# Taking the products of constants out of TensorE's waits in a two-block transformer kernel

## The reference, cut to what matters

```python
def hybrid_layer(xl, xc, ...):            # li = 0 with both streams, li = 1 ends the context stream
    hl = rmsnorm(xl, norm1_g) * (1 + sc1) + sh1
    # projections, q/k/v, rope ...
    a_l = mla_latent(...)                  # 6 heads
    b_l = swa_latent(...)                  # 6 heads
    xl = xl + g1 * (concat([a_l, b_l, cv_l]) @ w_o)
    xl = xl + g2 * ec_ffn(rmsnorm(xl, norm2_g) * (1 + sc2) + sh2, router_w, w_gate, w_up, w_down)

def ec_ffn(h, router_w, w_gate, w_up, w_down):
    aff = softmax(h @ router_w)            # 256 tokens x 16 experts
    top_aff, idx = lax.top_k(swapaxes(aff, 1, 2), 32)   # each expert picks its 32 tokens
    xg = h[idx]
    hid = silu(xg @ w_gate) * (xg @ w_up)
    # (hid @ w_down) * top_aff, added back to the tokens that were picked
```

## Time and profile before

| what | us |
|---|---|
| median of 3 runs | 2224.35 |
| lowest, highest | 2220.94, 2224.48 |
| the profiled execution | 2227.25 |
| its span, from the first to the last instruction | 2225.5 |
| TensorE busy in the span | 2066.0 (93%) |
| granted clock, mean over the span | 0.972 |

### The profile page before, as it was taken

The page is one execution under the profiler, slowest core; times in us unless marked ns, Lnnn a source line. Parts: engine busy times, 40 slices in busy tenths (PEclk is TensorE's granted clock), DMA queues, the critical chain, the costliest instruction groups (busy, mean ns, idle before and its releaser), DMA issues.

```text
span 2225.5 us, 32706 instructions
## 1 busy us (share of the span) xinstructions
PE 2066.0 (93%) x14137; PEld 1603.4 (72%) x14137; DVE 917.5 (41%) x1882; ACT 447.4 (20%) x984; POOL 86.3 (4%) x87
## 2 busy tenths in 40 slices
PE   6999999999899998667999999999999998999998
PEld 3444586555565476545878878899987788889998
DVE  2137723232326632113445423466514544146662
ACT  3004512111122421001223112100003411121001
POOL 1000010000000000000001100000000011000000
PEclk9999999999999999779999999999999999999999
DMA  9750633999922879997432214455543221244462
GB/s 369 250 202 25 211 127 118 395 424 426 400 77 78 303 296 388 416 416 291 148 107 103 76 64 142 148 178 158 159 151 121 97 93 68 86 151 165 157 166 82
DMA packets 186768, 435.69 MB, mean 196 GB/s; under 512 B 6362, under 2 KB 77954, under 8 KB 171010
## 3 DMA queue, kind: packets, MB, share of 16 engines
q1 hardware_dynamic: 185488, 431.19, 52.7%
q10 hardware_dynamic: 1138, 2.41, 0.3%
HBM read 432.53 MB, written 1.05 MB: 195 GB/s over the span
## 4 chain that ended last, share of the span: by engine, by line
PE 84%; DMA 8%; DVE 3%; ACT 2%; issue 1%; SPq 1%; DVEq 0%; ACTq 0%
PE bank L284 80%; DMA arena<-in_exp_w_up 3%; DMA ring<-in_exp_w_up 2%; PE bank L604 2%; PE bank L873 2%; DMA cst<-in_ada_w 1%; DMA ring<-in_exp_w_gate 1%; DMA cst<-in_exp_w_up 1%; SPq L3006 1%; ACT h L727 0%; ACT arena L827 0%; DVE arena L822 0%; PE bank L1452 0%; PE bank L1500 0%; DVE x L1381 0%
## 5 line engine op out<-in xcount | busy, mean ns | idle before, releaser
L284 PE MATMUL bank<-h,ring 128*128 128x256 f32 (+2 forms) x3360 | 744.6, 380 | 16.2 <-ACT arena L658 5.1
L284 PEld LDWEIGHTS bank<-h,ring 128*128 128x128 f32 x3360 | 595.5, 192 | 147.9 <-issue 68.3
L284 PE MATMUL bank<-arena 128*128 128x128 f32 (+13 forms) x3496 | 453.5, 328 | 40.4 <-DMA arena<-in_exp_w_gate 10.2
L284 PEld LDWEIGHTS bank<-arena 128*128 128x128 f32 (+5 forms) x3496 | 340.3, 171 | 131.4 <-issue 63.6
L284 PE MATMUL bank<-arena,ring 128*128 128x128 f32 (+1 forms) x1704 | 267.9, 317 | 1.0 <-PE bank L284 1.0
L284 PEld LDWEIGHTS bank<-arena,ring 128*128 128x128 f32 x1704 | 245.9, 191 | 19.6 <-PE bank L284 1.8
L827 ACT ACTIVATE arena<-bank 128x256 f32<-128x256 f32 (+4 forms) x227 | 100.5, 461 | 526.1 <-PE bank L284 497.2
L822 DVE COPY arena<-bank 128x512 f32<-128x512 f32 (+6 forms) x90 | 50.8, 566 | 242.0 <-PE bank L284 161.0
L284 PE MATMUL bank<-ring,arena 128*64 128x256 f32 (+1 forms) x1472 | 113.6, 348 | 20.8 <-DMA ring<-in_exp_w_up 13.3
L284 PEld LDWEIGHTS bank<-ring,arena 128*64 128x64 f32 (+1 forms) x1472 | 78.8, 130 | 58.1 <-DMA ring<-in_exp_w_up 16.8
L284 PE MATMUL bank<-h,arena 128*128 128x128 f32 (+2 forms) x704 | 109.9, 330 | 2.6 <-ACT arena L1491 2.6
(11 more groups left out here) (362 smaller groups left out, 1741.2 us busy)
## 6 DMA issues: line engine op xcount, KB each, us to landing
ring<-in_w_in SPq DMA_DIRECT2D x32, 2048.0 KB, 7.8
ring<-in_exp_w_up SPq DMA_DIRECT2D x19, 2048.0 KB, 13.4
ring<-in_ada_w SPq DMA_DIRECT2D x18, 2048.0 KB, 10.3
ring<-in_exp_w_gate SPq DMA_DIRECT2D x16, 2048.0 KB, 12.8
ring<-in_exp_w_down SPq DMA_DIRECT2D x16, 2048.0 KB, 16.0
ring<-in_w_ffn_gate SPq DMA_DIRECT2D x10, 2048.0 KB, 7.8
ring<-in_w_ffn_up SPq DMA_DIRECT2D x10, 2048.0 KB, 7.7
arena<-in_exp_w_down SPq DMA_DIRECT2D x9, 2048.0 KB, 18.0
```

Of the source, the lines that this page charges most:

```text
L284: return PE.matmul(o, lhsT, rhs, start=(k == 0), stop=(k == n - 1))
```

## The change

The three calls of `keep_busy` are taken out; the function stays, and nothing calls it.

```diff
                 mm(b[:, 0:384], ckv[:, 0, j * P:(j + 1) * P], wv, 0, 1).then_inc(*tensor.mark("v_mla", l, j))
-            keep_busy(pe, 2)
             join(tensor, pe, ("heads", l))
...
             last.then_inc(*tensor.mark("affT", l))
-            keep_busy(pe, 5)
             pe.wait_ge(*vector.at("pos", l))
...
                 mean_tensor(pe, NS * S, after_moe(l))
-                keep_busy(pe, 5)
             join(tensor, pe, ("moe", l))
```

## The result

The changed kernel takes 2230.51 us (median of 8 runs) against 2223.30 of the kernel before: a ratio of 1.0035, 95% interval 1.0020 to 1.0050. It is slower by 7.2 us, where 4.65 were forecast. Its profiled execution took 2234.78 us, 4.3 above its median; the profiled execution of before lies 3.95 above that of its eight runs, so the two can be compared piece by piece, but no single piece need be the typical one.

A forecast was written before the change was run, and what follows sets the result against it. TensorE's chain was taken as the bound (84% of the span). Terms 2.0 + 1.45 + 0.75 + 0 - 1.0 gave +3.2 us on the profiled execution; +4.65 on the median gave 2229.0, range 2224.5 to 2233.0.

The forecast's parts named there:

- Ahead of the attentions: Start of both attentions: without dummies TensorE pauses 4.03 us, not 2.14, and the clock falls; +2.0, bounds +1.7 and +4.4.
- Layer 1's term: Layer 1's attention scores: a new low clock costs at least 1.70, at most 2.70 us; taken as +2.0.
- Layer 0's term: Layer 0's attention scores: clock low already in the profile, so 0, bounds 0 and +1.70 us.
- Layer 0's routing: Hold-up of `posT` goes, -0.55; gathers pay the low clock, +2.0; sum +1.45 us, bounds +1.1 and +2.9.
- Layer 1's routing: Hold-up of `posT` goes, -1.45; gathers and first expert pay +2.2; sum +0.75 us, bounds +0.25 and +1.95.
- Behind the experts: Behind layer 0's experts: ScalarE's pace hides the low clock; 0, bounds 0 and +0.45 us.
- The banks: Second block's gate tile no longer waits for the reciprocal, -0.81; end's banks -0.2; sum -1.0 us, bounds -1.2 and 0.
- Does a shift pass?: Experts' loads: streams start on TensorE's releases of slots, so a routing that ends later shifts everything behind it.
- The size on the median: Whole kernel: +3.2 us against the profiled execution, up to +6.35 without its two unlucky pieces; +4.65 put on the median.
- the first (the clock is no matter): Gathers of both routings run at full clock from their start; only hold-ups and bank count: -3.0 us, 2221.3; chance 0.10.
- The second, that the loads hide the routings: Experts' streams end where they did; only attentions and bank stay: +1.8 us, 2226.2; chance 0.18.
- The third, +8.25 by low stretches that last: Each of the four places pays its upper bound: +8.25 us, 2232.6; chance 0.15.

The follow-up runs named there:

- x1_heads: Only the dummies ahead of both attentions left out of the kernel before, their bank still taken; ratio 1.0007 (2224.89 against 2224.44 us).
- z4_after_tail: The changed kernel with five products of constants added in the waits at the end of layer 0's attention; ratio 1.0028 against the kernel before (2229.82 us).
- y_after: The changed kernel itself run once more, against the kernel before; ratio 1.0027 (2229.73 against 2223.46 us).
- x2_routing: Only the dummies in the two routings left out of the kernel before, the bank still taken; ratio 1.0012 (2227.62 against 2224.44 us).
- x7_best: Kernel before with 16 records ahead of attentions, 16 and 12 in routings, none behind layer 0's experts, second block's banks as changed; ratio 0.9998 (2222.99 us).
- z3_best_tail: x7_best with five products of constants at the end of layer 0's attention; ratio 0.9979 against the kernel before (2218.90 against 2223.68 us).
- x4_turns: All the dummies left out of the kernel before, each place still taking its bank; ratio 1.0033 (2232.00 against 2224.44 us).
- z1_tail: The kernel before with five products of constants added in the waits at the end of layer 0's attention; ratio 1.0007 (2225.23 against 2223.68 us).
- x5_cover: The kernel before with 16 records of dummies instead of 8 ahead of both attentions; ratio 1.0022 (2228.80 against 2223.46 us).
- x6_trim: The kernel before with routing dummies cut from 20 records each to 16 in layer 0 and 12 in layer 1; ratio 0.9998 (2224.64 us).

## Why the prediction was right, and where it was not

The forecast was 2229.0, the measured medians are 2230.51 and 2229.73, within the range of 2224.5 to 2233.0 and on the side that it gave the higher chance, if barely (0.49 against 0.47). As a shift it is further off: +4.65 against +7.2 and +6.3. The first is even above the +6.35 that the prediction has as the forecast's upper end; the time lies closer because it was added to a median of three runs, 2224.35, which is 1.05 above that of eight. The steps in their order:

- **Ahead of the attentions, +2.0.** Layer 1's term is confirmed in mechanism and size: a pause of 3.86 us, PEclk 0.50 behind it, 1.70 us more in two profiles of the changed kernel, 2.72 in x1_heads and 2.90 in z4_after_tail. The bound of 2.70 was wrongly worked out: records that take 5.39 us at full clock take 10.78 at half, so the bound should have been 5.39. Layer 0's 8.78 us in the first profile, 3.39 above the full clock's 5.39, shows it passed. Layer 0's term was 0 with an upper bound of 1.70: it was 1.69 in the first profile, and 0.00 and 0.08 in y_after and z4_after_tail. What the prediction missed is that before loses these 1.70 us in layer 1 itself at times (in two of the five profiles with its dummies); x1_heads alone gave a ratio of 1.0007.
- **Layer 0's routing, +1.45.** `posT` came 0.55 us sooner behind `pos`, as worked out, though the row from out to the gathers fell by 0.23 to 0.31 only. The low clock in the gathers cost 2.88 and 1.42 us in the two profiles of the changed kernel and 3.05 in z4_after_tail, against 2.0 taken and 3.4 as bound. The taken value's weakness is that the low stretch had no fixed length: the gathers met its last 5.84 us in the first profile and 3.75 in x2_routing.
- **Layer 1's routing, +0.75.** Of the hold-up 1.46 went (1.45 worked out), and 2.07, 1.96 and 2.12 came back in the low clock (2.2 taken). The net of the first profile is 2.07 - 1.58 = +0.5, near the forecast. But before's profile was a late one here, as the prediction says: the row from out to the first up is 1.5 us longer without the dummies than with them, as means of five and six profiles.
- **Behind the experts, 0.** Right: 105.88 us in both profiles, although PEclk was 0.50 from 625.48 to 632.30. ScalarE's pace hid it.
- **The banks, -1.0.** Right: -1.04 and -0.16 in the profile, with the wait gone. From the reciprocal to the residual it takes 62.20 or 62.21 us in all five profiles with the new banks, two of which have dummies (x7_best, z3_best_tail), and 63.25 in all nine with the old ones. In the time it can't be told apart: x4_turns, without it, has 1.0033 and the changed kernel 1.0035 and 1.0027.
- **Does a shift pass?** Mostly. Behind layer 0's routing all of it did in the first profile (+0.38 more), and the last landing of the experts' weights moved with it: 219.24 us behind the first gate, where it was 218.82. From the first up of layer 1 to the reciprocal the changed kernel gained 1.57 us; that piece differs by several us between kernels that don't differ in it (in z1_tail and y_after, too, it is below that of before), and nothing here settles why.
- **The size on the median, +4.65.** The median moved by 7.2 and 6.3 us. The weak step is the way from the profiled execution to the median, by two pieces that are called unlucky. The low clock at layer 0's scores was not luck: all five profiles with those eight records have 7.33 or 7.34 us to the transposes, so there was no 1.70 to add. The late `posT` of layer 1 was luck for about half (0.10 to 1.63 us in six profiles). And at layer 1's scores before's profile was a lucky one (7.17, where two of five have 8.87). A third place, the end of layer 0's attention, was not in the sum at all. It made +5.22 of the first profile; z4_after_tail, which covers it, has the median of y_after, so these runs don't show it in the median.
- **What the profiles add up to.** Taken as means, the profiles without a place's dummies less those with them (five each at the scores, five and six in the routings) give +0.36 at layer 0's scores, +1.59 from out to the first gate of layer 0, +1.46 at layer 1's scores and +1.48 from out to the first up of layer 1; with -1.05 for the banks that is +3.8. So the terms of the forecast have their signs and, but for layer 1's routing (0.75 forecast), about their sizes, and some 2.4 to 3.4 us of the median's shift stand in no piece that is shown to be the change's. Where they lie stays open: the row from the first up of layer 1 to the reciprocal alone runs from 494.1 to 501.9 us in the fourteen profiles, and the end of layer 1's attention, where the clock is low for 3.4, 6.8 or 10.2 us in every one of them, from 58.5 to 61.7. That 4.65 came as near as it did is in part luck.

Of the rivals the first (the clock is no matter) is refuted: the gathers began at 0.50 in every profiled execution without dummies ahead of them. The second, that the loads hide the routings, doesn't go with x2_routing, whose last landings moved and whose interval, 1.0004 to 1.0021, lies above 1. The third, +8.25 by low stretches that last, is near the first profile's +7.5, but not by its reason: 5.22 of that stand at a place that it does not name. The rule of the Trainium skill that was named there (TensorE: Matmul & The Clock Gate, Part 4: PE-mode transpose) gets no support: the attentions of x5_cover keep the full clock from 191.50 to 273.90 with transposes between the scores.

The price of a low stretch is the best confirmed number. It costs half of what is left of it when useful products begin: 5.84 / 2 = 2.92 against 2.88 measured, 3.75 / 2 = 1.87 against 1.85, 4.31 / 2 = 2.16 against 2.07. The Trainium skill has the same half (TensorE: Matmul & The Clock Gate, HAM oscillation — how this bites in real kernels): there the penalty is the throttled time times one minus the ratio of the two clocks. The traces agree within 0.13 us at all ten starts of gathers without dummies ahead of them, if only the low time behind the gathers' start is counted.

## What to carry to other kernels

Products of constants in a wait paid where they left TensorE only a short pause ahead of useful products (x5_cover's scores: 0.41 us, full clock, 1.70 won). Where they end late, they give in hold-up what they save in clock (the routings of before); trimmed, they kept the full clock with 0.23 us left ahead of `posT` (x6_trim, layer 0), and did not with 1.09 us left (layer 1). Price a low clock as half of the low time that falls on useful products, and look for it at all places with pauses, also unchanged ones: a gain at one place can be lost at another (x5_cover), and only covering the place that fell as well made a quicker kernel (z3_best_tail, 0.9979). Take several profiled executions of the same kernel before a piece of a few us is called the change's, or the luck of one execution: here 5.22 of 7.5 us were one execution's.

## What the hardware showed that was not expected

Pauses far shorter than the 2.14 us ahead of the scores were enough for the granted clock to fall to half. It fell 0.2 to 0.6 us after TensorE had begun again behind the first of the four, of 0.81 us: at 277.32 in the changed kernel's first profile (products from 277.08), at 273.90 in x5_cover (from 273.26) and at 274.78 in x7_best (from 274.23). Just ahead of that pause TensorE ran eight records of 12 columns, in 1.06 us; whether they have a part in the fall is not shown. In the 70 us ahead no pause was longer than 0.57 us; the other three of the four, of 1.17, 0.61 and 0.56 us, came behind the fall. In the seven other profiles without products in these waits the very same pauses left the clock at 1.00. What differed was when they came: the products behind the first pause began between 275.03 and 276.50 in the seven, and earlier or later in the three. Why that decides, these runs don't show. The Trainium skill has a like case (TensorE: Matmul & The Clock Gate, A second HAM failure mode: psum-queue depth-cycling): frequent small pauses between groups of products made the clock go back and forth. The trace agrees that no single long pause is needed, and with five products in the waits, which left pauses of 0.28, 0.31, 0.18 and 0.56 us, it stayed at 1.00 there in the profiles of all four kernels that had them.

The wait of 2.14 us ahead of layer 1's scores is the other case of this kind: with the same dummies the scores took 7.17 us to the transposes in the kernel before and 8.87 in x2_routing.
